# Moving weight splits, head squares and page sums inside a hybrid decoder's attention jobs

## What is computed

```python
h = _rmsnorm(xp, attn_pre_g[l])
q1, q2, ka, va, qf, kf, vf, logf = _project(h, w_in[l], b_f[l], pos_p)   # with rotation of q1, q2, ka
cf = jnp.cumsum(logf, axis=1)
oa, of = _prompt_attention(q1, q2, ka, va, qf, kf, vf, cf, lam)
#   oa = (softmax(q1 k1^T) - lam softmax(q2 k2^T)) v     4 differential heads, two maps each
#   of = softmax(q k^T + cf[t] - cf[s]) v                8 forgetting heads
xp = xp + _rmsnorm(_merge(oa, of, subln_g[l], lam_init, w_o[l]), attn_post_g[l])
#   _merge: RMSNorm of each differential head (128 wide), then one projection
xp, conv_p = _conv_ffn(xp, prev0, ...)
...
gather = lambda c: c[l][page_table].reshape((DB, past_len) + c.shape[3:])
# the same for xs over gathered pages: scores q . k of every page, softmax, weighted sum of value pages
```

## Time and profile before

| | us |
|---|---|
| three executions | 1506.09, 1511.02, 1512.67 (median 1511.02) |
| the profiled execution | 1511.48, span 1509.7 |
| TensorE busy | 1442.5 (96% of the span) |
| VectorE, ScalarE, GpSimd busy | 862.5 (57%), 636.9 (42%), 370.2 (25%) |
| mean granted clock of TensorE | 0.983 of full speed |
| from issue to landing, key pages (256 KB each half) | 2.9 and 3.1 (medians) |

### The profile page before, as it was taken

The page is one execution under the profiler, slowest core; times in us unless marked ns, Lnnn a source line. Parts: engine busy times, 40 slices in busy tenths (PEclk is TensorE's granted clock), DMA queues, the critical chain, the costliest instruction groups (busy, mean ns, idle before and its releaser), DMA issues. The chain is left out here.

```text
span 1509.7 us, 26823 instructions
## 1 busy us (share of the span) xinstructions
PE 1442.5 (96%) x10396; PEld 1297.5 (86%) x10396; DVE 862.5 (57%) x1378; ACT 636.9 (42%) x1194; POOL 370.2 (25%) x548
## 2 busy tenths in 40 slices
PE   7999989999998999889999999999999999999998
PEld 6999777767767677468789999999999999999998
DVE  6412566565554546465547876666776646444673
ACT  6723555544354434443332633323333324343543
POOL 5213876764654442032100000000000000000120
PEclk9999999999999999899999999999999999999999
DMA  5213546666755654622223222222222236655773
GB/s 183 56 35 92 176 153 220 213 209 227 240 174 181 199 181 124 202 85 71 71 84 93 71 77 79 85 84 85 71 85 71 71 133 207 202 187 178 235 263 112
DMA packets 174840, 209.91 MB, mean 139 GB/s; under 512 B 22051, under 2 KB 118891, under 8 KB 174676
## 3 DMA queue, kind: packets, MB, share of 16 engines
q1 hardware_dynamic: 174714, 208.21, 43.6%
HBM read 178.37 MB, written 29.88 MB: 138 GB/s over the span
## 5 line engine op out<-in xcount | busy, mean ns | idle before, releaser
L629 POOL TENSOR_TENSOR k_page<-k_page,q_bc 128x256 f32<-128x256 f32 x256 | 186.9, 762 | 130.3 <-DMA k_page<-in_cache_fox_k 102.8
L1205 PE MATMUL PS<-ht_hi,w_hi 128*128 128x344 f32 x576 | 196.5, 341 | 6.3 <-POOL w_lo L600 3.3
L1205 PE MATMUL PS<-ht_hi,w_lo 128*128 128x344 f32 x576 | 186.8, 324 | 0.0
L1205 PE MATMUL PS<-ht_lo,w_hi 128*128 128x344 f32 x576 | 186.7, 324 | 0.0
L2435 PE MATMUL PS<-act_hi,wd_hi 128*128 128x344 f32 x528 | 169.2, 321 | 2.6 <-DVE act_lo L2270 2.6
L2435 PE MATMUL PS<-act_hi,wd_lo 128*128 128x344 f32 x528 | 168.8, 320 | 0.0
L2435 PE MATMUL PS<-act_lo,wd_hi 128*128 128x344 f32 x528 | 168.6, 319 | 0.0
L838 ACT ACTIVATE probs<-probs,stat 128x256 f32<-128x256 f32 (+7 forms) x128 | 98.7, 772 | 137.6 <-DVE stat L1082 137.3
L2267 DVE TENSOR_TENSOR wd_lo<-wd_raw,wd_hi 128x1024 fp32r<-128x1024 f32 (+1 forms) x88 | 85.8, 978 | 112.2 <-ACT act_hi L2078 92.3
L1205 PEld LDWEIGHTS PS<-ht_hi,w_hi 128*128 128x128 f32 x576 | 111.3, 193 | 32.1 <-issue 25.1
L2075 ACT ACTIVATE wd_hi<-wd_raw 128x1024 fp32r<-128x1024 f32 (+1 forms) x88 | 74.2, 844 | 139.1 <-DMA act_raw<-a_dram 102.5
(11 more groups left out here) (280 smaller groups left out, 3319.5 us busy)
## 6 DMA issues: line engine op xcount, KB each, us to landing
wd_raw<-in_w_down SPq DMA_DIRECT2D x44, 512.0 KB, 3.5
k_page<-in_cache_diff_k SPq DMA_DIRECT2D x64, 256.0 KB, 2.9
k_page<-in_cache_fox_k SPq DMA_DIRECT2D x64, 256.0 KB, 3.1
v_page<-in_cache_diff_v SPq DMA_DIRECT2D x64, 256.0 KB, 2.8
v_page<-in_cache_fox_v SPq DMA_DIRECT2D x64, 256.0 KB, 3.1
w_raw<-in_w_in SPq DMA_DIRECT2D x24, 512.0 KB, 4.6
a_dram<-conv SPq DMA_DIRECT2D x22, 516.0 KB, 3.1
act_raw<-a_dram SPq DMA_DIRECT2D x66, 172.0 KB, 3.7
```

Source lines behind the costliest of these rows:

```text
L629: ins = pool.tensor_tensor(kpage[:, g % 2, c:c + PIECE], kpage[:, g % 2, c:c + PIECE], qbc[:, c:c + PIECE], ALU.mult)
L1205: ins = pe.matmul(PS[0:rows, z_bank(c), 0:THIRD], b[:, k, :], a[:, k, third(i)], start=(k == 0 and p == 0), stop=(k == KC - 1 and p == 2))
```

## The change

In GpSimd's loop the first page of a job goes ahead of `split_lo` and a second one behind it, and in jobs up to 3 the rotations go ahead of both. In ScalarE's loop both weight splits stand behind `turned` and ahead of `exponentials`; `head_squares` stands there too, with a job number one higher than before, so that only the `a_t` copies (and the copy `o_part`) pass it. `late_page` names the second page of a job with two (unless it is a sequence's last) and each sequence's first page from page 8 on; these are summed behind `weights` in the job two after their own, instead of at the end of the job after it, and the load that takes their slot stands one job later on SyncE's queue.

```diff
+    ROPE_FIRST = 3
+    late_page = lambda g: g > EARLY_PAGES and (g % PAGES == 0 or k_job(g) == k_job(g - 1) and g % PAGES < PAGES - 1)
...
-                    if max(0, k_job(g - 2) + 1) == J:
+                    if max(0, k_job(g - 2) + 1 + late_page(g - 2)) == J:
...
+                ropes = [c for c, h in fill(J - 1)[0] + fill(J - 1)[1] if h] if J else []
+                if J <= ROPE_FIRST:
+                    for c in ropes:
+                        rope(c)
                 n = {1: k_tile(u + 1) + 1, 5: k_tile(u + 2)}.get(t, len(TILES))
-                if n < len(TILES):
-                    split_lo(n)
-                for g in k_pages(J):
+                for g in k_pages(J)[:1]:
                     if g % PAGES == PAGES - 1:
                         later_pages(g // PAGES)
                     multiply(g)
-                if J:
-                    for c, h in fill(J - 1)[0] + fill(J - 1)[1]:
-                        if h:
-                            rope(c)
+                if n < len(TILES):
+                    split_lo(n)
+                for g in k_pages(J)[1:]:
...
+                if J > ROPE_FIRST:
+                    for c in ropes:
+                        rope(c)
...
-                n = k_tile(u + 1) + 1
-                if t == 1 and n < len(TILES):
-                    split_hi(n)
                 if J >= 2:
                     turned(J - 2)
...
+                for v in range(NT):
+                    if norm_job(v) + 1 == J:
+                        if v == 0:
+                            act.wait_ge(norm_sems["zeroed"], 1)
+                        head_squares(v)
+                n = {1: k_tile(u + 1) + 1, 5: k_tile(u + 2)}.get(t, len(TILES))
+                if n < len(TILES):
+                    split_hi(n)
                 if J < NJ:
                     exponentials(J)
...
+                for g in k_pages(J - 2):
+                    if late_page(g):
+                        reduce_page(g)
                 if 2 <= J < NJ + 2 and not fox(J - 2):
                     rows_out(J - 2)
```

More of the change, by code:

```diff
@@ L682, in _ @@
                     multiply(g)
-                if J:
-                    for c, h in fill(J - 1)[0] + fill(J - 1)[1]:
-                        if h:
-                            rope(c)
+                if n < len(TILES):
+                    split_lo(n)
+                for g in k_pages(J)[1:]:
+                    if g % PAGES == PAGES - 1:
+                        later_pages(g // PAGES)
+                    multiply(g)
+                if J > ROPE_FIRST:
+                    for c in ropes:
+                        rope(c)
                 if J == 4 * NT + 2:
@@ L893, in _ @@
                     act.activation(scores[:, b % 3], scores[:, b % 3], ACT.Exp).then_inc(e_done, 1)
[L894 to L898, removed]
                 if J == NJ - 5:
@@ L906, in _ @@
                     act.activation(pair[0:DB, :, :], pair[0:DB, :, :], ACT.Exp).then_inc(new_exp, 1)
-                n = k_tile(u + 2)
-                if t == 5 and n < len(TILES):
-                    split_hi(n)
         @block.vector
@@ L1143, in _ @@
                 for g in range(2, EARLY_PAGES) if J == 0 else k_pages(J - 1):
-                    reduce_page(g)
+                    if not late_page(g):
+                        reduce_page(g)
                 for b in at_job(J, 1):
```

## The result

The changed kernel takes **1519.23 us** (median of 21 runs, 1511.41 to 1528.05), the kernel before 1510.21 in 21 runs beside it. The ratio is 1.0065, 95% interval 1.0051 to 1.008: slower by two thirds of a per cent, and outside the forecast range of 1491 to 1508. The profiled execution took 1526.48 us with a span of 1524.7, seven above its median, so the profile shows 15 us of loss where the medians show 9.

What follows compares the result with a forecast made beforehand. TensorE was taken as the bound, with 46.8 us idle inside the jobs to win; gains and losses summed to 15.1 us, less 1.7 for a new half-clock stretch, 13.4, giving 1498 us, range 1491 to 1508.

Steps and rivals of the forecast that it cites:

- The step that failed: On SyncE's queue, loads into late first pages' slots move one job later; value pages loaded two ahead cover the few us.
- Together -2.7: Late first-page sums ahead of `rows_out` lose 1.2 us each in jobs 6 and 13, 0.3 in job 20, elsewhere nothing.
- So page 28 is multiplied from 317.50: Job 23: ScalarE's late w_hi delays GpSimd's w_lo and its page product; TensorE then stands 3.49 us for VectorE's weights.
- Second pages: Late sums in jobs 7, 15, 23, 31: gains 2.2, 3.0 of half clock and 1.6; job 7 loses 0.6.
- ScalarE: Splits and squares behind the `a_t` copies: waits gain 9.3 us, half clock 1.7; late exponentials cost 1.0.
- rival (c): ScalarE's squares ahead of exponentials cost as much as behind them, 8 x 1.4 us lost; 1508 us, chance 0.08.
- GpSimd's other orders: Earlier w_lo in job 45 gains 1.2 us in job 46 plus 1.7 half clock; rotations first in job 3 gain 0.8.
- Given back: Chains that start at a DMA keep the `q_t` waits in jobs 40 and 48, returning 2.1 us of other gains.
- Rival (b): Moved sums block `rows_out` because GpSimd's products come later than the weights in seven differential jobs; 1520 us, chance 0.06.
- Rival (a): Late sums and DMA chains take gains back: jobs 7, 15, 23, 31 keep their waits; 1506 us, chance 0.20.
- The clock rule: Every TensorE stall removed takes its share of half clock along, and none comes anew; 1492 us, chance 0.04.
- The signs: Right: no `a_t` wait above 0.5 us, job 23 at most 1.5; wrong: VectorE waiting at moved sums, `probs` waits over 1.5.

Runs made afterwards that it cites:

- the fastest one: Changed kernel with only second pages and page 56 late, its successor's load ahead of value loads, head statistics early in jobs 38 and 46: 1483.0 us, 0.9837.
- the early statistics: Kernel with only second pages late, plus head statistics ahead of GpSimd's pages (jobs 38, 46) and `head_norm` behind VectorE's weights (39, 47): 1488.51 us, 0.9862.

## Why the prediction was wrong, point by point

**The step that failed** is the one on first pages: "On SyncE's queue the load of the page that takes the late page's slot goes one job on, and value loads and row stores of the next job stand behind it; value pages are loaded two ahead, which covers the few us." I had asked what stands behind the moved load, and not what it now stands behind. A value load two ahead means that SyncE waits in it for TensorE, for up to 9.0 us in the kernel before, and the key load had been just ahead of it. The queue's order alone costs 18 us (1519.2 against 1501.3 with the load ahead and 1501.7 with it unmoved).

**Its price**, "Together -2.7", "in job 27 ... and the forgetting jobs do `rows_out` at their start: nothing": I priced only the sum's own 1.2 us in front of `rows_out`. The runs give 31 us for first pages alone and 22.6 on top of late second pages (1519.2 - 1496.7; 22.5 by the ratios), about half of it in the forgetting jobs. I had seen the mechanism once, at page 10 in job 7, and charged it 0.6 us there; I didn't carry it to jobs 15, 29, 43 and 50, where the same slot rule holds. Nor did I see that GpSimd's page-first order makes w_lo wait with the page (8 to 9 us, by the run with its loop as before). The 18 and the 9 overlap: with the load ahead, job 43's wait for w_lo is gone too.

**A reading that was wrong.** "So page 28 is multiplied from 317.50" laid the lateness of job 23's second page to w_hi and w_lo. The row says that the product waited 1.48 us for the page's DMA, and with w_lo moved out of the way it still does (1.27 us, job 23 stalls 3.53). What mended job 23 was the late sum: with late sums and loads alone it waits 0.73 us.

**Second pages** were right in kind and size: job 23 waits 0.73 us for `q_t` at full clock, where the sum had 1.3 and the same clock. The terms 2.2 + 3.0 + 1.6 - 0.6 = 6.2 stand beside 7.7 measured at job 32, but 5 us of it are given back by job 63, which the sum did not have. Job 15's 2.1 us for `q_t` in the change itself go back to the first page 16: page 18 comes late, page 19 behind it, and page 19's moved sum waits 1.3 us for its product ahead of `rows_out`; with second pages alone job 15 waits 0.7.

**ScalarE** was right: no `a_t` wait above 0.5 us between 415 and 560, 12.4 us for the 10.8 of the sum. A cost of late exponentials doesn't show in the 12.4, so rival (c), which would have left 10 us less, is out.

**GpSimd's other orders**: TensorE waits 2.08 us for w_lo in job 3 where the sum had 1.9, and the part alone gives nothing (0.8 forecast; its interval goes from 2 us faster to 3.6 slower). In job 46 the wait for `lf_after` went as forecast.

**Given back**: jobs 40 and 48 still wait, as the prediction asked, 2.8 and 5.9 us. The chain from q_bc was named rightly but undersized: of the 3.8 us that jobs 46 and 47 win with ScalarE's part alone, job 48's wait takes back 3.05 (2.07 became 5.12), where the sum let 2.3 of 4.4 stay. "Taking a page sum out ahead of `head_norm` wins nothing, because `head_norm` waits for the same chain" holds only while the head statistics stand behind the page on GpSimd; with them ahead, the chain can be cut. (A small slip besides: the sum's last step takes the 13.4 from the profiled 1511.48; from the median it would be 1497.6.)

**The rivals.** Rival (b), given 0.06, has the time, 1520, but not by its mechanism: of the twelve moved sums eleven wait for nothing and page 19's waits 1.3 us; it's the ordinary sums of the pages that take their slots that wait, 2.4 to 7.1 us each (18, 26, 34, 42, 50, 58). That its time fits is luck. Rival (a) is out as stated: with second pages late alone the `probs` waits of jobs 7 to 31 fall from 9.9 to 0.9 us. The clock rule (1492) is out as a time, since new stalls came. In the run with first pages alone 6.1 us of stall stand ahead of 0.50 from 275 to 280, and of the profile's loss in the change as made the lower clock made as much as the idle time itself, 7.8 beside 7.2 us. By the Trainium skill (TensorE: Matmul & The Clock Gate, "HAM oscillation"), idle gaps cost the full clock for the work behind them; the trace agrees.

**The signs.** Every sign of being right came true: no `a_t` wait, 0.73 us for `q_t` in job 23, 2.1 and 1.0 us for `q_t` in jobs 6 and 13, 2.8 and 5.9 us in jobs 40 and 48. Of the signs of being wrong only page 19's 1.3 us showed. The loss came in jobs 29, 43 and 50, which no sign named, and in job 48, where "over 2 us" let 5.9 pass. A limit on the waits of all jobs together would have caught it.

In medians, one part put in after the other: 1510.2 - 12.4 (ScalarE) + 1.2 (GpSimd) - 2.4 (second pages) + 22.6 (first pages) = 1519.2. The sum closes by construction, and each term holds for this order; of them the 1.2 and the 2.4 are within the noise.

## What to carry to other kernels

When a DMA moves on an in-order queue, list what it now stands *behind*, with what each of those waits for, before listing what stands behind it; an early prefetch that waits for a slot is a gate for everything after it. Releasing a slot later delays every later tenant of it, so follow the slot two pages on to the first consumer that isn't moved as well. And put into a queue first what somebody waits for: small statistics ahead of the page whose input comes late were worth 8 us here.

## What the hardware showed

VectorE's `head_norm`, four instructions of 128x128, took 1.13 us with GpSimd idle (job 40) and 3.00 us beside a GpSimd product (job 48), both in the kernel before; in the fastest one, again with GpSimd idle, it took 1.12 (505.14 above):

```profile
453.31 1.13 DVE L1100 SCALAR_TENSOR_TENSOR q_t<-q_t,head_stat,g_sub 128x128 f32<-128x128 f32 x4
...
527.93 2.92 POOL L629 TENSOR_TENSOR k_page<-k_page,q_bc 128x256 f32<-128x256 f32 x4
527.99 3.00 DVE L1100 SCALAR_TENSOR_TENSOR q_t<-q_t,head_stat,g_sub 128x128 f32<-128x128 f32 x4
```

That is a factor of 2.7, far more than the 1.51 against 1.15 us of the weights, and it may be part of the 8 us that the early statistics gave (in job 47 of that run `head_norm` takes 1.12 us, in job 48 of the run with second pages alone 3.00); no run separates it. The Trainium skill (SBUF — State Buffer, "Who interferes with whom") says that a VectorE instruction with two SBUF inputs contends with a GpSimd instruction that reads SBUF; the rows agree.

The changed kernel's 21 runs spread over 17 us (1511 to 1528), the 21 of the kernel before, taken beside them, over 9.5. What spreads them stays open.
